# Input rows of 1280 bytes in place of 1088 for the stages with 272 columns

## The reference

```python
def hgrn2_mix(h, g_norm, w_in, g_out, w_out, lb):        # h: 272 x 2048
    u = rms_norm(h, g_norm) @ w_in                        # 2048 -> 4 * 2048
    ...
    return (o * silu(z)) @ w_out                          # 2048 -> 2048
def fox_shared_kv(h, g_kv, w_kv, b_f, g_k):               # h: 272 x 2048
    u = rms_norm(h, g_kv) @ w_kv                          # 2048 -> 2 * 2048 + 16
...
# expert layer, 256 tokens, all 16384 experts
h = einsum("cd,chkd->chk", xc, u_sel)                     # the up stage
y = einsum("chk,chkd->cd", gelu(h) * gates, v_sel)        # the down stage
```

## Time and profile before

| | us |
|---|---|
| median of three executions | 3037.82 |
| lowest and highest of them | 3034.54, 3038.83 |
| the profiled execution | 3035.7 |
| its span, first to last instruction | 3033.6 |
| TensorE busy with matmuls | 2998.9 (99%) |
| VectorE, ScalarE, GpSimd busy | 1949.0, 1611.8, 654.0 |

### The profile page before, as it was taken

One profiled execution on the slowest core, in us unless ns is written; L12 is line 12 of the kernel. 1 busy time (PEld: TensorE's weight loads), 2 busy tenths in 40 slices (PEclk: granted clock), 3 DMA queues, 4 the chain that ended last, 5 costly groups with the idle time before them and its releaser, 6 DMA issues.

```text
span 3033.6 us, 63446 instructions
## 1 busy us (share of the span) xinstructions
PE 2998.9 (99%) x25230; PEld 2942.8 (97%) x25230; DVE 1949.0 (64%) x3289; ACT 1611.8 (53%) x2603; POOL 654.0 (22%) x289
## 2 busy tenths in 40 slices
PE   9999999999999999989999999999999999999999
PEld 8999998999999998879999999999999999999999
DVE  6777776644544568767777798555448865555444
ACT  6777675566788643455444444444444444444443
POOL 3333333444444432104444300000000000000000
PEclk9999999999999999999999999999999999999999
DMA  5444443544444454325555544555554455555554
GB/s 207 152 152 146 145 152 130 178 166 166 167 139 143 149 186 151 113 98 182 179 183 181 181 151 156 192 183 192 185 189 160 154 189 181 192 181 194 184 190 166
DMA packets 72432, 506.67 MB, mean 167 GB/s; under 512 B 7920, under 2 KB 10480, under 8 KB 11504
## 3 DMA queue, kind: packets, MB, share of 16 engines
q1 hardware_dynamic: 71728, 503.16, 48.4%
q10 hardware_dynamic: 576, 1.72, 0.2%
HBM read 502.75 MB, written 2.10 MB: 166 GB/s over the span
## 4 chain that ended last, share of the span: by engine, by line
PE 95%; DVE 3%; ACT 1%; issue 0%; DMA 0%; SPq 0%; DVEq 0%; ACTq 0%
PE bank L451 13%; PE bank L450 12%; PE bank L452 12%; PE bank L464 6%; PE bank L2327 4%; PE banks L2327 4%; PE bank L2328 4%; PE banks L2328 4%; PE bank L2329 4%; PE banks L2329 4%; PE bank L2100 3%; PE bank L2101 3%; PE bank L2102 3%; PE banks L2100 3%; PE banks L2101 3%; PE banks L2102 3%
## 5 line engine op out<-in xcount | busy, mean ns | idle before, releaser
L427 ACT ACTIVATE whi<-raw 128x1024 fp32r<-128x1024 f32 x896 | 941.0, 1057 | 989.5 <-PE bank L452 366.5
L434 DVE TENSOR_TENSOR wlo<-raw,whi 128x1024 fp32r<-128x1024 f32 x671 | 856.2, 1287 | 429.2 <-ACT whi L427 428.2
L434 POOL TENSOR_TENSOR wlo<-raw,whi 128x1024 fp32r<-128x1024 f32 x227 | 596.9, 2630 | 941.7 <-ACT whi L427 930.0
L450 PE MATMUL bank<-xa_hi,whi 128*128 128x272 f32 (+1 forms) x1984 | 576.6, 291 | 4.0 <-DVE wlo L434 3.8
L451 PE MATMUL bank<-xa_lo,whi 128*128 128x272 f32 (+1 forms) x1984 | 568.3, 286 | 0.0
L452 PE MATMUL bank<-xa_hi,wlo 128*128 128x272 f32 (+1 forms) x1984 | 567.2, 286 | 0.0
L450 PEld LDWEIGHTS bank<-xa_hi,whi 128*128 128x128 f32 x1984 | 373.6, 188 | 6.3 <-issue 4.7
L451 PEld LDWEIGHTS bank<-xa_lo,whi 128*128 128x128 f32 x1984 | 374.8, 189 | 1.3
L452 PEld LDWEIGHTS bank<-xa_hi,wlo 128*128 128x128 f32 x1984 | 373.7, 188 | 0.0
L450 PE MATMUL bank<-xb_hi,whi 128*128 128x256 f32 (+1 forms) x1120 | 317.4, 283 | 1.5 <-DVE wlo L434 1.5
L451 PE MATMUL bank<-xb_lo,whi 128*128 128x256 f32 (+1 forms) x1120 | 315.9, 282 | 0.0
(11 more groups left out here) (460 smaller groups left out, 6771.5 us busy)
## 6 DMA issues: line engine op xcount, KB each, us to landing
raw<-in_w SPq DMA_DIRECT2D x250, 1024.0 KB, 4.8
raw<-in_v SPq DMA_DIRECT2D x128, 1024.0 KB, 5.2
raw<-in_u SPq DMA_DIRECT2D x96, 1024.0 KB, 4.8
hT<-in_hT SPq DMA_DIRECT2D x4, 544.0 KB, 7.4
out<-hT SPq DMA_DIRECT2D x8, 256.0 KB, 2.3
raw<-in_w SPq DMA_DIRECT2D x2, 512.0 KB, 6.6
r_keys<-in_keys ACTq DMA_DIRECT2D x1, 1024.0 KB, 5.1
c_mask<-in_masks ACTq DMA_DIRECT2D x1, 320.0 KB, 2.8
```

Source lines behind the costliest of these rows:

```text
L427: act.activation(whi[:, (2 * t.q + half) % 4, :], raw[:, t.q, half * 1024:(half + 1) * 1024], ACT.Copy).then_inc(w_hi_done, 1)
L434: eng.tensor_tensor(wlo[:, t.q, at], raw[:, t.q, at], whi[:, slot, :].bitcast(F32), ALU.subtract).then_inc(w_lo_done[half], 1)
L450: te.matmul(ps, hi, x[0][:, kk, cols], start=(kk == 0), stop=False)
```

## The change

`xa` stays for the stages with 256 columns. For `hgrn_tensor` and `kv_tensor` a second pair, `xw`, is laid over the same space. Its rows are 320 floats long (1280 bytes, 5 x 256) of which 272 are used, so all 16 rows of a tensor have the same place modulo 256. A gap of 224 bytes ahead of `xw_hi` puts it at 224, and one of 32 bytes puts `xw_lo` at 0. With 64 floats behind them the pair takes 6656 bytes more than `xa`, so the tensors of `g`, `f` and `c` move by 6656 bytes.

```diff
+WIDE = 320
...
-        xa = (tensor(innermost, "xa_hi", [P, KT, L], F32R), tensor(innermost, "xa_lo", [P, KT, L], F32R))
+        with ExitStack() as st:
+            xa = (tensor(st, "xa_hi", [P, KT, L], F32R), tensor(st, "xa_lo", [P, KT, L], F32R))
+
+        def wide(name, gap):
+
+            tensor(innermost, f"{name}_gap", [P, gap])
+            room = tensor(innermost, name, [P, KT * WIDE], F32R)
+            return room.rearrange("p (k w) -> p k w", k=KT)[:, :, 0:L]
+
+        xw = (wide("xw_hi", 56), wide("xw_lo", 8))
+        tensor(innermost, "xw_rest", [P, 64])
...
-        OUT = ((T_AOUT, xb, cols_all, "kv_norm", xa, 1), (T_BOUT, xa, cols_q, "norm1", xn1, 3),
+        OUT = ((T_AOUT, xb, cols_all, "kv_norm", xw, 1), (T_BOUT, xa, cols_q, "norm1", xn1, 3),
...
-                    te.matmul(ps, hi, xa[0][:, kk, :], start=(kk == 0), stop=False)
-                    te.matmul(ps, hi, xa[1][:, kk, :], start=False, stop=False)
-                    last = te.matmul(ps, lo, xa[0][:, kk, :], start=False, stop=(kk == KT - 1))
+                    te.matmul(ps, hi, xw[0][:, kk, :], start=(kk == 0), stop=False)
+                    te.matmul(ps, hi, xw[1][:, kk, :], start=False, stop=False)
+                    last = te.matmul(ps, lo, xw[0][:, kk, :], start=False, stop=(kk == KT - 1))
```

More of the change, by code:

```diff
@@ L692, in body @@
                 elif within(h, HEADS):
-                    project(te, t[0], xa, cols_all)
+                    project(te, t[0], xw, cols_all)
                 if within(h - 2, HEADS):
@@ L707, in body @@
                 if within(h, HEADS):
-                    project(te, t[1], xa, cols_all)
+                    project(te, t[1], xw, cols_all)
                 if static(h) and h == HEADS:
@@ L725, in body @@
                 if within(h, HEADS):
-                    project(te, t[2], xa, cols_all)
+                    project(te, t[2], xw, cols_all)
                 if static(h) and h == HEADS:
@@ L744, in body @@
                 if within(h, HEADS):
-                    project(te, t[3], xa, cols_all)
+                    project(te, t[3], xw, cols_all)
                 if static(h) and h == HEADS:
@@ L760, in hgrn_scalar @@
                 for kk in range(4 * k, 4 * k + 4):
-                    act.activation(xa[0][:, kk, :], hT[:, kk, :], ACT.Copy, scale=par("a_norm", kk))\
+                    act.activation(xw[0][:, kk, :], hT[:, kk, :], ACT.Copy, scale=par("a_norm", kk))\
                         .then_inc(x_hi_done, 1)
@@ L850, in hgrn_vector @@
                 ve.wait_ge(x_hi_done, k + 1)
-                ve.scalar_tensor_tensor(xa[1][:, k, :], hT[:, k, :], par("a_norm", k), xa[0][:, k, :].bitcast(F32),
+                ve.scalar_tensor_tensor(xw[1][:, k, :], hT[:, k, :], par("a_norm", k), xw[0][:, k, :].bitcast(F32),
                                         ALU.mult, ALU.subtract).then_inc(x_split, 1)
@@ L964, in body @@
                     if static(h) and h == 0:
-                        project(te, Tile(T_KV, i, 0), xa, cols_all, halves=(0,))
+                        project(te, Tile(T_KV, i, 0), xw, cols_all, halves=(0,))
                         out_sum(te, T_AOUT, L)
-                        project(te, Tile(T_KV, i, 0), xa, cols_all, halves=(1,))
+                        project(te, Tile(T_KV, i, 0), xw, cols_all, halves=(1,))
                     elif within(h, HEADS):
-                        project(te, Tile(T_KV, i, 2 * u), xa, cols_all)
+                        project(te, Tile(T_KV, i, 2 * u), xw, cols_all)
                     if within(h, HEADS):
-                        project(te, Tile(T_KV, i, 2 * u + 1), xa, cols_all)
+                        project(te, Tile(T_KV, i, 2 * u + 1), xw, cols_all)
                         te.wait_ge(ksq_done, h + 1)
@@ L977, in kv_tensor @@
             ch.run(body, 0, HEADS // 2, 0)
-            project(te, Tile(T_FORGET, 0, 0), xa, cols_all)
+            project(te, Tile(T_FORGET, 0, 0), xw, cols_all)
         def kv_scalar(act, ch):
```

## The result

The changed kernel takes 3040.82 us (median of 20 executions, 3039.12 to 3044.03), the kernel before 3036.01 in the same comparison (20 executions, 3034.54 to 3039.03). The ratio is 1.0015 with an interval of 1.0009 to 1.0021: the change makes the kernel 4.8 us slower. Less than 0.2%, but in the other direction than forecast.

The account below looks back on a forecast made before the run. TensorE, 95% of the chain, was taken to bound the kernel through its matmul pitches. The four executions' mean of 3036.7 us less 4.2 for the matmuls, with writes and moved tensors at 0, gave 3032.5 us; range 3026 to 3041.

Parts of the forecast that it names:

- What bounds the kernel: Whole kernel: TensorE makes up 95% of the chain; in the two touched stages shorter matmul pitch becomes shorter time one to one.
- That the place matters: Down stage: input place modulo 256, not the stage, changes the step; first tile at 0 takes 357 ns against 349.
- Rival B: Two 272-column stages: no effect, length sets the loss and the fixed place gives 375.7 ns a step; 3036.7 us; chance 0.12.
- Taking over the difference at 256 columns: 272-column matmuls: the 2.7 ns a step between up and down stages carries over, 373.0 ns, 4.2 us less over 1552 steps.
- The upper end: 272-column matmuls: fixed place as bad as 0 is at 256 columns, 5.4 ns a step above turning rows, 8.4 us more.
- rival C: Two 272-column stages: slower, row's end spoils the place, 5.4 ns a step more; +8.4 us, 3045.1 us; chance 0.12.
- The writes: ScalarE and VectorE copies into the new place: no dearer, taken as 0; bound 0.8 us if first 16 take 10% more.
- The moved tensors: `g`, `f` and `c`: 6656 is 26 x 256, so they keep their place modulo 256; 0.
- What comes behind: Drain at 483 to 500 us: earlier end shifts the clock dip, up to 1.7 us either way; no new wait.

Follow-up runs that it names:

- 0/128: Kernel before with the low input starting at 128 modulo 256, not 0 (high at 0, 1088-byte rows turning by 64, changed kernel's addresses behind): 3035.84 against 3037.59 us, ratio 0.9995.

## Why the prediction was wrong

*What bounds the kernel*: right. The two stages grew by 3.7 and 2.1 us with TensorE at 444.24 of 444.30 us, and nothing beside it moved the end.

*That the place matters*: right, and confirmed at 256 columns inside the touched stages. Rival B (no effect) falls with it, at 380.00 against 375.83 ns.

*Taking over the difference at 256 columns* is **the step that failed**. It put 2.7 ns less on each of 1552 steps; measured are 4.2 ns more (380.00 - 375.83). The argument was that the part which length brings "probably stays" as it was for turning rows, some 4 ns (31.6 to 35.7). At the fixed place length brings 9 to 11 ns (28.9 in the down stage, 29.2 and 30.9 here, to 40.0), and the run with 264 columns shows all of it by the eighth column past 256. A difference between two layouts at one length was carried to another length, where it has the other sign: each length and layout has step times of its own.

*The upper end*, 5.4 ns a step more, did hold the measured 4.2, and with it rival C the sign: 1552 x 4.2 = 6.5 us by the steps, 5.8 in the two stages, 4.8 in the median. Of the signs named, C's step near 381 is the one that came. Its mechanism did not hold. C had the high input's row ending at a bad place; the trace has the loss between the start of B, on the low input, and that of C, and moving the low input gave the loss to A and C. That 3040.82 still lies within the 3026 to 3041 of the forecast is luck: that end was B with the spread of executions, and B did not happen. The chance of 0.12 for C looks too low. The rows had shown a fixed place above and one below the turning rows, and for 272 columns neither; that was evidence for a spread, not for the better of the two.

*The writes*: right. The copies into `xw_hi` take 508 ns in the second stage, against 507, and the first 16 of them 510 against 509.

```profile
L571 ACT ACTIVATE xw_hi<-hT,params 128x272 fp32r<-128x272 f32 x16 | 8.1, 508 | 0.0
```

*The moved tensors*: right; with turning rows and the same move the steps were 375.7 and 373.3 ns and the time 3034.77 us.

*What comes behind*: right in part. The drain behind the first stage grew by 0.75 us (28.20 to 28.95), within the 1.7 allowed. But the dip near 10 us (+1.05) and the ones around 1280 to 1372 us moved too, and the prediction had neither. What makes 4.8 us in the medians of the 5.8 in the stages is not shown. From the rule of two independent read ports in the Trainium skill ("SBUF — State Buffer", "Who interferes with whom") rival B took that no place would matter; 373.3 to 380.0 ns for one and the same work contradict that.

What stays open: what in the chip has the grain of 6.67 ns, and why a given layout settles as it does. That places count modulo 256 was taken from the start on and is not tested by itself. The step times were measured, not foreseen; of the two numbers worked out ahead from single pitches, 373.3 never came in the run it was for, apart from one of the two kv tiles left out, and 380.0 in 13 of 63 tiles of one stage.

## What to carry to other kernels

A difference of a few ns in a matmul's pitch between two stages belongs to their whole setting, number of columns included; before a layout is copied from one stage to another, it is to be measured at the length where it will be used. Where matmuls and weight loads run back to back, read the time of several steps and not single pitches, and of many tiles: a saving on one matmul came back on the next here, and one layout had other step times in other tiles.

## What the runs showed of the hardware

- Eight steps come out in whole grains of 6.67 ns wherever all tiles of a stage agree: 444 (2960.0 ns), 448, 450, 451, 452, 453, 454 and 456 (3040.0). One layout can settle in two of them, 376.7 and 380.0 ns a step in tiles of one stage. Where tiles differ, eight steps need not be whole grains: 0/128 has 2985 to 2986 and 3002 to 3003 ns.
- Which of its values a tile takes is no chance: in the two executions of 0/128 all tiles of the first stage from the 13th on have the same to within 1 ns, in an order that repeats every four tiles.
- The grain runs through the whole execution. In the kernel before, the start times of A modulo 6.67 ns, averaged over eight steps of a tile, were taken from the 254 tiles between 25 and 2670 us whose eight steps are 3006 or 3007 ns (272 columns), or 2813 or 2814 (256). They lie on a straight line with a drift of 1.6 ns in 1000 us to within 0.6 ns, all but two to within 0.35, with one constant for 272 and one for 256 columns, though other work lies between the tiles.
- VectorE's remainder of the weights in the first stage fell from 1771 to 1246 ns on average (63 each, the same instruction on the same tensors), while GpSimd's part of the same work rose from 2623 to 2885, as the groups from the first tile's end to the stage's end show, before and after. In the fourteen traces VectorE's mean is 1769 to 1772 in the nine with a first-stage step of up to 376.7 ns, and 1246 to 1560 in the five with 377.4 ns and more. It does not make the step's time: in the kv stage it is 1216 ns in all fourteen, while the step with 272 columns goes from 373.3 to 380.0 there. Why it changes, no run tested.

```profile
L434 DVE TENSOR_TENSOR wlo<-raw,whi 128x1024 fp32r<-128x1024 f32 x63 | 111.6, 1771 | 0.0
L434 POOL TENSOR_TENSOR wlo<-raw,whi 128x1024 fp32r<-128x1024 f32 x63 | 165.2, 2623 | 272.6 <-ACT whi L427 272.6
```

```profile
L445 DVE TENSOR_TENSOR wlo<-raw,whi 128x1024 fp32r<-128x1024 f32 x63 | 78.5, 1246 | 0.0
L445 POOL TENSOR_TENSOR wlo<-raw,whi 128x1024 fp32r<-128x1024 f32 x63 | 181.7, 2885 | 259.7 <-ACT whi L438 259.7
```
